# Wider matmuls in the expert loop: one 512-column product over both parts of the state, and merged gate pieces

## What is computed

```python
def peer_ffn(x, w_q, sub_keys, u, v):
    ...
    gate = jax.nn.softmax(top_s, axis=-1)
    ...
        hid = jax.nn.gelu(jnp.einsum('btd,bthkd->bthk', xb, u[eb]).astype(jnp.float32), approximate=False)
        w = (gb * hid).astype(x.dtype)
        return jnp.einsum('bthk,bthkd->btd', w, v[eb])
```

## Time and profile before

| | us |
|---|---|
| median of 3 runs | 2198.21 (2195.53 to 2203.95) |
| profiled execution | 2195.7, its span 2193.8 |
| PE busy | 2109.5 of the span |
| DVE busy | 1540.7 |
| ACT busy | 952.5 |
| POOL busy | 856.7 |

### The profile page before, as it was taken

How to read it: one execution, slowest core, us unless ns; L and a number is a source line. 1 busy time by engine, 2 the same in 40 slices (tenths; PEclk the granted TensorE clock), 3 DMA queues, 4 the chain that set the end, 5 groups by cost and what they waited for, 6 DMA issues and landing times.

```text
span 2193.8 us, 46574 instructions
## 1 busy us (share of the span) xinstructions
PE 2109.5 (96%) x18012; PEld 1922.2 (88%) x18034; DVE 1540.7 (70%) x2683; ACT 952.5 (43%) x1399; POOL 856.7 (39%) x360
## 2 busy tenths in 40 slices
PE   6989988999999999999989999899999999999998
PEld 6978988888989898999888789898898989899997
DVE  5572698998876887566354618989887777776663
ACT  5563434334444444433555534343434343433444
POOL 4624640004343434444555257300034343434444
PEclk9999999999999999999999899999999999999999
DMA  6403443444444444455443034434444444445553
GB/s 236 154 20 136 157 152 112 158 153 172 172 172 173 172 172 172 176 187 191 159 166 137 4 134 157 150 117 155 156 171 174 171 174 171 172 172 190 185 181 113
DMA packets 48523, 342.62 MB, mean 156 GB/s; under 512 B 5536, under 2 KB 6560, under 8 KB 7200
## 3 DMA queue, kind: packets, MB, share of 16 engines
q1 hardware_dynamic: 47984, 337.93, 43.0%
q10 hardware_dynamic: 432, 3.21, 0.4%
HBM read 340.08 MB, written 1.05 MB: 155 GB/s over the span
## 4 chain that ended last, share of the span: by engine, by line
PE 87%; DVE 5%; ACT 3%; issue 2%; POOL 2%; DMA 1%; SPq 0%; DVEq 0%; ACTq 0%; POOLq 0%
PE psum L448 26%; PE psum L449 25%; PE psum L450 25%; PE psum L766 4%; POOL wl L372 1%; ACT wh L360 1%; DMA ring<-stream 1%; PE psum L462 1%; PE psum L667 1%; DVE wl L372 1%; PE psum L591 1%; PE psum L738 1%; ACT arena L887 1%; PE psum L659 1%; DVE arena L1630 1%
## 5 line engine op out<-in xcount | busy, mean ns | idle before, releaser
L372 POOL TENSOR_TENSOR wl<-ring,wh 128x1024 fp32r<-128x1024 f32 x336 | 831.9, 2496 | 1277.0 <-ACT wh L360 1277.0
L360 ACT ACTIVATE wh<-ring 128x1024 fp32r<-128x1024 f32 x628 | 627.7, 1046 | 396.4 <-PE psum L450 384.0
L448 PE MATMUL psum<-xh,wh 128*128 128x256 f32 (+1 forms) x2320 | 668.6, 288 | 13.2 <-DVE wl L372 12.2
L449 PE MATMUL psum<-xl,wh 128*128 128x256 f32 (+1 forms) x2320 | 659.5, 284 | 0.0
L450 PE MATMUL psum<-xh,wl 128*128 128x256 f32 (+1 forms) x2320 | 659.4, 284 | 0.0
L448 PEld LDWEIGHTS psum<-xh,wh 128*128 128x128 f32 (+1 forms) x2320 | 446.6, 192 | 18.5 <-issue 14.0
L449 PEld LDWEIGHTS psum<-xl,wh 128*128 128x128 f32 (+1 forms) x2320 | 446.9, 193 | 1.3
L450 PEld LDWEIGHTS psum<-xh,wl 128*128 128x128 f32 (+1 forms) x2320 | 446.7, 193 | 0.2
L372 DVE TENSOR_TENSOR wl<-ring,wh 128x1024 fp32r<-128x1024 f32 x292 | 362.2, 1280 | 100.8 <-ACT wh L360 100.8
L448 PE MATMUL psum<-wh,Wh 128*128 128x512 f32 (+1 forms) x1056 | 412.5, 391 | 3.7 <-POOL Wl L1204 2.0
L449 PE MATMUL psum<-wl,Wh 128*128 128x512 f32 (+1 forms) x1056 | 408.7, 387 | 0.0
(11 more groups left out here) (229 smaller groups left out, 2119.1 us busy)
## 6 DMA issues: line engine op xcount, KB each, us to landing
ring<-stream SPq DMA_DIRECT2D x318, 1024.0 KB, 4.8
arena<-keys ACTq DMA_DIRECT2D x2, 1024.0 KB, 6.7
smr<-rows SPq DMA_DIRECT2D x1, 1090.0 KB, 11.0
smr<-rows ACTq DMA_DIRECT2D x1, 1090.0 KB, 5.2
h<-x SPq DMA_DIRECT2D x1, 1024.0 KB, 5.0
out<-h SPq DMA_DIRECT2D x4, 256.0 KB, 2.1
sm<-cols SPq DMA_DIRECT2D x1, 728.0 KB, 9.0
kst<-consts SPq DMA_DIRECT2D x1, 495.0 KB, 7.7
```

The costliest lines, as they stand in the source:

```text
L360: nc.scalar.activation(wh[:, buffer_of(L, n), c], ring[:, (L * SLOTS + n) % RING, c], ACT.Copy).then_inc(hi_ok, 1)
L372: eng.tensor_tensor(wl[:, b, c], ring[:, (L * SLOTS + n) % RING, c], wh[:, b, c].bitcast(F32), ALU.subtract).then_inc(done, 1)
L448: pe.matmul(o, a[0], b[0], start=start, stop=False, **kw)
L449: pe.matmul(o, a[0], b[1], start=False, stop=False, **kw)
```

## The change

The state's two parts become one tile `xx`, `[xh | xl]` side by side for each feature block. In quarters 1 to 3, for pairs 17 to 63 (47 pairs a layer), the U product is `hidden_wide`: the high part of U times both parts of the state in one matmul of 512 columns, and the low part of U times the high part of the state in one of 256. The result of one expert row now fills a whole bank, 4 or 5, so a pair takes both banks: in the left half what belongs to the high part of the state, in the right half what belongs to the low part. The halves are summed by two more operations: ACT copies the right halves to SBUF (`gelu_wide`, first activation), DVE adds the copy to the left halves in PSUM (`halves_added`), and then ACT takes the Gelu. The wait of `hidden_wide` for the Gelu is now for the pair just before.

The gate steps in quarters 1 and 2 (for the gates of quarters 2 and 3) become `spread_wide`: 16 matmuls of 64 columns that leave the two pieces apart in both banks 6 and 7. ACT copies one piece out as before and DVE adds the other (`pieces_added`).

DVE's order in the pair loop changes: low half 0 of V of p, one-hots, `halves_added` of p+1, low half 1 of V of p, `weigh(p+1)`, `pieces_added`.

```diff
-        xh = sb("xh", [P, DC, SEQ], F32R)
-        xl = sb("xl", [P, DC, SEQ], F32R)
+        xx = sb("xx", [P, DC, 2, SEQ], F32R)
+        xh, xl = xx[:, :, 0, :], xx[:, :, 1, :]
...
+        def summed(j):
+            return psum[:, 4:6, j * SEQ:(j + 1) * SEQ]
+        def both_pieces():
+            return psum[:, 6:8, :].rearrange("p b n -> p (b n)").rearrange("p (t k e) -> p k e t", k=PIECES, e=QI)
...
+                def spread_wide(n, par):
+                    pe.wait_ge(b_ok, n + 1)
+                    pe.wait_ge(a_ok, n + 1)
+                    for i in range(TB):
+                        ins = pe.matmul(bank(6 + 2 * i // TB, PIECES, QI, at=i % (TB // 2) * PIECES * QI), Bh[:, par, i, :],
+                                        Ah[:, par, :, i, :], start=True, stop=True)
+                    ins.then_inc(g_ps, 1)
...
+                def hidden_wide(i, p):
+                    w = [a.rearrange("p (e k n) -> p e k n", e=2, k=DC) for a in parts(L, u_slot(p))]
+                    pe.wait_ge(gelu_ok, L * PAIRS + 2 * i + p)
+                    for e in range(2):
+                        half(L, u_slot(p), e, i)
+                        for k in range(DC):
+                            pe.matmul(bank(4 + e, 512), w[0][:, e, k, :], xx[:, k, :, :].rearrange("p a t -> p (a t)"),
+                                      start=(k == 0), stop=False, skip_group_check=True)
+                            ins = pe.matmul(bank(4 + e, SEQ), w[1][:, e, k, :], xh[:, k, :], start=False, stop=(k == DC - 1),
+                                            skip_group_check=True)
                     ins.then_inc(slot_used, 1)
...
                             p = quarter * QP + k
-                            hidden(i, p + 1)
+                            hidden_wide(i, p + 1)
                             weighted(i, p)
                             if quarter < QUARTERS - 1:
-                                spread(q0 + (quarter + 1) * NB + 2 * i + k, k)
-                hidden(0, PAIRS - 1)
+                                spread_wide(q0 + (quarter + 1) * NB + 2 * i + k, k)
+                hidden_wide(0, PAIRS - 1)
...
+                def gelu_wide(i, p):
+                    used(act, L, u_slot(p) + 4 * i)
+                    act.wait_ge(w_ok, L * PAIRS + 2 * i + p - 1)
+                    g = GL[:, p % 2, :].rearrange("p (e t) -> p e t", e=2)
+                    act.activation(g, summed(1), ACT.Copy).then_inc(hc_ok, 1)
+                    if not isinstance(i, int) or p < PAIRS - 1:
+                        high_half(L, u_slot(p + 1), i, 0)
+                    act.wait_ge(hs_ok, L * (PAIRS - QP - 1) + 2 * i + p - QP)
+                    act.activation(g, summed(0), ACT.Gelu).then_inc(gelu_ok, 1)
+                    if not isinstance(i, int) or p < PAIRS - 1:
+                        high_half(L, u_slot(p + 1), i, 1)
...
-                                   bank(6 + n % 2, TB, QI).rearrange("p t e -> p e t"),
+                                   (bank(6 + n % 2, TB, QI).rearrange("p t e -> p e t") if quarter < 2 else both_pieces()[:, 0]),
...
-                            gelu(i, p + 1)
-                            high(L, u_slot(p + 2), i)
+                            gelu_wide(i, p + 1)
                             high(L, v_slot(p + 1), i)
...
+                def low_part(i, p, j):
+                    low_half(dve, L, v_slot(p), i, j, vlo_ok)
+                def halves_added(i, p):
+                    n = L * (PAIRS - QP - 1) + 2 * i + p - QP
+                    dve.wait_ge(hc_ok, n)
+                    dve.tensor_tensor(summed(0), summed(0), GL[:, p % 2, :].rearrange("p (e t) -> p e t", e=2),
+                                      ALU.add).then_inc(hs_ok, 1)
...
+                def pieces_added(quarter, i, n):
+                    dve.wait_ge(g_ok, (L * QUARTERS + quarter) * NB + 2 * i + n + 1)
+                    buf = ar((quarter % 2) * SEQ * QI, QI, SEQ)[:, :, bass.ds((2 * i + n) * TB, TB)]
+                    dve.scalar_tensor_tensor(out=buf, in0=both_pieces()[:, 1], scalar=1.0 / G_SCALE, in1=buf,
+                                             op0=ALU.mult, op1=ALU.add).then_inc(gm_ok, 1)
...
-                for quarter in range(1, QUARTERS):
-                    dve.wait_ge(g_ok, (L * QUARTERS + quarter + 1) * NB)
-
-                    def body(i):
-                        for k in range(2):
-                            weigh(i, quarter * QP + k)
-                            low(i, quarter * QP + k)
-                            if quarter < QUARTERS - 1:
-                                ahead(quarter, i, k)
+                dve.wait_ge(g_ok, (L * QUARTERS + 2) * NB)
+                weigh(0, QP)
+                for quarter in range(1, QUARTERS - 1):
+                    def body(i, ks):
+                        for k in ks:
+                            low_part(i, quarter * QP + k, 0)
+                            ahead(quarter, i, k)
+                            halves_added(i, quarter * QP + k + 1)
+                            low_part(i, quarter * QP + k, 1)
+                            weigh(i, quarter * QP + k + 1)
+                            pieces_added(quarter + 1, i, k)
                     with dve.Fori(0, QP // 2 - 1) as i:
-                        body(i)
-                    if quarter < QUARTERS - 1:
-                        body(QP // 2 - 1)
-                for p in (PAIRS - 2, PAIRS - 1):
-                    weigh(0, p)
-                    low(0, p)
+                        body(i, range(2))
+                    body(QP // 2 - 1, range(1))
+                    low_part(0, (quarter + 1) * QP - 1, 0)
+                    ahead(quarter, QP // 2 - 1, 1)
+                    halves_added(0, (quarter + 1) * QP)
+                    low_part(0, (quarter + 1) * QP - 1, 1)
+                    pieces_added(quarter + 1, QP // 2 - 1, 1)
+                    dve.wait_ge(gm_ok, (2 * L + quarter) * NB)
+                    weigh(0, (quarter + 1) * QP)
+                with dve.Fori(0, QP // 2 - 1) as i:
+                    for k in range(2):
+                        low_part(i, (QUARTERS - 1) * QP + k, 0)
+                        halves_added(i, (QUARTERS - 1) * QP + k + 1)
+                        low_part(i, (QUARTERS - 1) * QP + k, 1)
+                        weigh(i, (QUARTERS - 1) * QP + k + 1)
+                low_part(0, PAIRS - 2, 0)
+                halves_added(0, PAIRS - 1)
+                low_part(0, PAIRS - 2, 1)
+                weigh(0, PAIRS - 1)
+                low(0, PAIRS - 1)
```

More of the change, by code:

```diff
@@ L335, in trunk @@
         b_ok, e_ok, a_ok, g_ps, g_ok = (sem(n) for n in ("b_ok", "e_ok", "a_ok", "g_ps", "g_ok"))
+        gm_ok, hc_ok, hs_ok = sem("gm_ok"), sem("hc_ok"), sem("hs_ok")
         gelu_ok, w_ok, acc_ps = sem("gelu_ok"), sem("w_ok"), sem("acc_ps")
@@ L779, in hidden @@
                                           [xh[:, k, :], xl[:, k, :]], k == 0, k == DC - 1)
+                    ins.then_inc(slot_used, 1)
+                def hidden_wide(i, p):
[8 more added lines that the diff above has]
+                                            skip_group_check=True)
                     ins.then_inc(slot_used, 1)
@@ L1081, in gelu @@
                     used(act, L, u_slot(p) + 4 * i)
-                    if p < QP:
-                        out_ = lead_slot(step * i + p)
-                    else:
-                        if p > QP:
-                            act.wait_ge(w_ok, L * PAIRS + step * i + p - 1)
-                        out_ = GL[:, p % 2, :]
+                    out_ = lead_slot(step * i + p) if p < QP else GL[:, p % 2, :]
                     src = bank(4 + p % 2, 512)
@@ L1140, in _ @@
                                 gates_out(quarter + 1, i, k)
-                gelu(0, PAIRS - 1)
+                gelu_wide(0, PAIRS - 1)
                 high(L, v_slot(PAIRS - 1))
```

## The result

The changed kernel takes 2182.66 us (median of 7 runs, 2176.05 to 2188.61); the kernel before, beside it, takes 2195.53 (7 runs, 2190.53 to 2203.95). The ratio is 0.9942 with an interval of 0.9922 to 0.9962. A second set of runs gave 2180.86 against 2195.75, 0.9930 (0.9915 to 0.9945). So the change is a gain of 0.6 to 0.7%, small but clear, where I had forecast none. The profiled execution took 2185.45 us with a span of 2183.7.

A forecast was written before the change was run, and what follows sets the result against it. PE was taken to bound the kernel; -15 (quarters 1 and 2), +3 (quarter 3) and +14 (lost races) gave +2 on the profiled 2195.7, which ran 2.5 below the median, so 2199 us; range 2180 to 2245.

The forecast's parts named there:

- +2 for the stages: Whole kernel: -15 for quarters 1 and 2, +3 for quarter 3, +14 for lost races, on the profiled 2195.7 us.
- the loop's turn: Pair loop on PE, quarter 1: 0.09 us a pair on average kept on top of PE's 11.57.
- wait in V: Before V's 13th matmul: PE waits for low half 1, queued behind copy and sum; 0.30 us a pair, bounds 0.2 and 0.45.
- Prices of the matmuls: On PE: U product saves 0.21 us in each of 94 pairs, gate step 0.34 in each of 64; 42 us in all.
- the Trainium skill's rule: Matmul gap of columns over 2.4 plus 2.5 ns; U products would save 4 us in place of 20.
- Quarter 1's start: First V product of quarter 1: POOL starts first, low half 1 comes too late, +2.5 us.
- From quarter 1 to 2: Turn of quarters: weighing waits for the last `pieces_added`, low half 0 late by 0.9, low half 1 by 3; some +3.8 us.
- Quarter 3, +0.09 a pair: Quarter 3 pairs: U product saves 0.21, wait in V costs 0.30; over 30 pairs +3 us.
- The race in the steady state: Rival, 20%: in quarters 1 and 2 POOL starts ahead of DVE's low half, 2.55 us each; 2240 to 2280 us.
- the stages' +14: Lost races at quarter 1's start and the quarters' turns, 6.8 us a layer; bounds 0 and 20.

The follow-up runs named there:

- gates only: Kernel before plus only the merged gate step (16 matmuls of 64 columns, pieces added by DVE), U products unchanged: 2171.81 us, ratio 0.9891 to the kernel before.
- U products only: Changed kernel with the gate step as before (32 matmuls of 32 columns, no add of pieces): 2199.44 us, ratio 1.0017 to the kernel before.
- two operations more: Changed kernel with two extra 0.33 us DVE operations on unread memory ahead of the sum of halves, quarters 1 and 2: 2281.81 us, ratio 1.0375.
- one operation more: Changed kernel with one extra 0.33 us DVE operation on unread memory ahead of the sum of halves, quarters 1 and 2: 2199.26 us, ratio 1.0021.

## Why the prediction was wrong

I forecast 2199 and no change; it is 2183, at the lower end of the range, and faster by more than the measurement's uncertainty. The sum had +2 for the stages; it was -13.4. (The sum itself was added up 1 low: 2195.7, +2 and +2.5 are 2200.) Two steps failed above all: 0.09 a pair kept for the loop's turn without a reason, and a wait in V of 0.30 that is 0.20. The steps, in their order:

- **Prices of the matmuls: right in quarters 1 and 2, wrong in quarter 3.** The gate step is 0.48 (0.47 forecast). The U product is 5.63 to 5.64 (5.62 forecast), which saves the 0.20 there. In quarter 3 it saves 0.11, because it took 5.75 there before, not 5.83; I had priced both from one row of quarter 2. On PE the wide form saves 16 us, not 20. By the Trainium skill's rule ("TensorE: Matmul & The Clock Gate", "Back-to-back issue gap") it would save 4; this trace doesn't agree.
- **"0.09 on average that I keep for the loop's turn": wrong, 6 us.** The gap is gone with the short gate step; gates only and U products only show that it is this edit's doing. I had measured the gate step where the loop doesn't turn, and had no reason for keeping the gap but that I couldn't explain it.
- **The wait in V, "I take 0.30 a pair": right in its place, too large by 0.10, 6 us in 64 pairs.** The chain is the one that I wrote, copy, sum, second low half, 13th matmul; but the low half ends 2.74 after V's start and not 2.83, since the sum follows the copy by 0.03 and not 0.1 or more, and PE follows the low half by 0.05, not by the 0.14 of the earlier trace rows. The 0.11 before the next matmul is the 0.08 that I had allowed. So the two distances are 0.15 longer and not 0.30. Another 0.05 a pair, spread over the matmuls behind, I didn't have, and it stays unexplained; it hides part of the error.
- **"Quarter 1's start ... low half 1 is too late: +2.5": wrong, 4 us.** It won by 0.14 (507.72 to 507.86), and the pair took 12.04 to 12.11. DVE came 0.4 earlier than I had it (508.1), POOL 0.3 later (507.55). With 0.33 us more on DVE it lost, and the pair took 14.37: the mechanism and the price stand, the side on which it fell doesn't. I should have priced it as a chance.
- **From quarter 1 to 2, "with both some +3.8": right but for the clock, which I had not put in, 3 us.** It is 5.2 a layer. The waits are in the places that I gave: PE stands 0.24 for the first low half and 3.03 for the second, and with what each costs around it that is near 3.6 beyond a usual pair. The other 1.6 is the granted clock, which fell behind the pause. In the sum this error and that of quarter 1's start all but cancel: the stages' +14 is 11.6.
- **Quarter 3, +0.09 a pair: 0.07, by luck.** I had -0.21 and +0.30; it is -0.11 and +0.18. Both terms were too large by about the same.
- **The race in the steady state (20%): didn't happen, and is real.** I gave it 0.3 to 0.45 of room; 0.33 more doesn't lose it and 0.66 does. The pair is then 14.4 as written, or 15.9 where the clock falls, and every second to third pair is one.

What it adds up to: 64 pairs by -0.09 (loop's turn) and -0.10 (wait in V) are -12, quarter 1's start -4.4, the turn from quarter 1 to 2 +2.8 (the clock), quarter 3 -1. That is some -15, by which +2 becomes about -13; measured is -13.4. Of the U products' 16 us on PE nothing arrives: the V products take 18 back. In quarters 1 and 2 the chain and DVE's order hold the pair at the 11.77 that the gates reach alone; in quarter 3 it is 0.07 longer than with the gates alone, and at the turn from quarter 1 to 2 the two halves together cost 5.2 a layer, where the gates alone cost 0.35 and the U products alone about 0.2.

What stays open: why the gap at the loop's turn needs 32 narrow matmuls, why a wide U product saves 0.20 behind a gate step and 0.11 without one, and the 0.05 in V.

## What to carry to other kernels

Price the halves of a change apart: here one alone was worth more than both, and the other paid only once the work on the engine behind it was moved too. When an instruction is put ahead of a prepared operand, write out the chain to the matmul that wants it, step by step, and take each handover from a row of the same two kinds of instruction where there is one; where a race for a shared port is near even, give it a chance and both prices. And before giving up a saving that is eaten by a full engine, look for an operation of it that an idle engine can take and a position in which its waiting costs nothing: the same wide products then brought some 15 us on top of the gates. And where a sum comes out right, look at its terms: in quarter 3 two wrong ones made it so.

## What the runs showed of the hardware

- One order of instructions has two stable rhythms, 11.58 and 12.43 to 13.12 us a pair, by who of DVE and POOL starts first. The Trainium skill ("SBUF — State Buffer", "Who interferes with whom") calls what they share an exclusive lock; the trace agrees: two operations that take 0.75 together took 2.95 behind a POOL operation that had started 0.43 before them.
- PE followed the end of a DVE instruction by 0.05 us at the 13th matmul of V and by 0.14 at a gate step; DVE followed ACT's copy by 0.03.
- A wait of 2.7 us on PE can be followed by some 3 us at a granted clock of 0.55 (620.30 to 623.50 with two operations more): such a pair took 15.9, others with the same wait 14.4. The changed kernel has one such stretch in each layer, behind the wait of 3.03.
- DVE's three operations behind the second low half take turns with POOL's two. Which of them wait depends on 0.3 us of position, and the sum of the waits hardly does: 4.2 a pair in the changed kernel, 4.1 with one operation more.
